# One attention kernel, heads taken in pairs: half-array products, transposed output rows, reciprocals spread by TensorE

## What is computed

```python
dots = einsum('bqhe,bse->bqhs', q_idx, k_idx)                 # indexer, 16 heads of 64
score = where(key_chunk <= q_chunk, sum_h w_h * relu(dots / 8), -inf)
_, sel = top_k(score, 256)
logits = einsum('bqhd,bqkhd->bqhk', q, k[sel]) * 64 ** -0.5   # 8 heads of 64
p = softmax(where(valid, logits, -1e30))
y_a = einsum('bqhk,bqkhd->bqhd', p, v[sel])
x = x + gt1 * (concatenate([y_a, y_b], -1) @ w_o)
h = rmsnorm(x, g_norm_ffn) * (1 + sc2) + sh2                  # then the router and the experts
```

## Time and profile before

| | |
|---|---|
| median of 3 runs | 1916.66 us (1916.6 to 1916.66) |
| the profiled execution | 1921.34 us |
| its span | 1919.2 us |
| TensorE busy | 1657.2 us (86%) |
| VectorE busy | 1389.6 us (72%) |
| ScalarE busy | 724.3 us (38%) |
| mean granted clock | 0.933 |
| attention, first query-key product to the last multiply by the reciprocals | 802.8 to 1186.1 us |

### The profile page before, as it was taken

How to read it: one execution, slowest core, us unless ns; L and a number is a source line. 1 busy time by engine, 2 the same in 40 slices (tenths; PEclk the granted TensorE clock), 3 DMA queues, 4 the chain that set the end, 5 groups by cost and what they waited for, 6 DMA issues and landing times.

```text
span 1919.2 us, 19711 instructions
## 1 busy us (share of the span) xinstructions
PE 1657.2 (86%) x6542; PEld 1090.3 (57%) x6542; DVE 1389.6 (72%) x1888; ACT 724.3 (38%) x819; POOL 170.6 (9%) x173
## 2 busy tenths in 40 slices
PE   2899999999999999468889998359999999999950
PEld 1346554444445545444555666248888888888840
DVE  6323776899778888886655322559999999999948
ACT  4000563000001001121332333037777777777733
POOL 0000000000111111100000000021101101101015
PEclk8899999999999999689999997669999999999985
DMA  9039202200100000672210101079999999999947
GB/s 363 1 132 377 111 1 88 82 14 36 44 6 6 6 12 6 222 257 99 78 49 17 44 28 44 22 291 423 422 411 414 414 412 415 414 414 411 400 161 257
DMA packets 85358, 355.29 MB, mean 185 GB/s; under 512 B 7984, under 2 KB 12208, under 8 KB 60720
## 3 DMA queue, kind: packets, MB, share of 16 engines
q1 hardware_dynamic: 56496, 268.51, 35.3%
q0 software_dynamic: 11776, 44.04, 6.2%
q10 hardware_dynamic: 17024, 41.95, 5.7%
HBM read 295.75 MB, written 58.72 MB: 185 GB/s over the span
## 4 chain that ended last, share of the span: by engine, by line
PE 45%; DVE 7%; ACT 2%; DMA 2%; issue 1%; POOL 0%; POOLq 0%; DVEq 0%; ACTq 0%
PE PS L1610 9%; PE PS L1612 9%; PE PS L1611 9%; PE PS L1572 5%; PE PS L1526 3%; PE PS L1516 3%; PE PS L1605 1%; PE PS L1546 1%; PE PS L1582 1%; DVE wlo L1295 1%; PE PS L1629 1%; ACT WK L730 1%; DVE WK L994 1%; DVE raw L1354 1%; DVE BIG L994 1%
## 5 line engine op out<-in xcount | busy, mean ns | idle before, releaser
L1295 DVE TENSOR_TENSOR wlo<-raw,whi 128x2048 fp32r<-128x2048 f32 x192 | 436.1, 2287 | 45.5 <-ACT whi L757 45.5
L757 ACT ACTIVATE whi<-raw 128x2048 fp32r<-128x2048 f32 x192 | 363.4, 1911 | 56.5 <-DVE WK L1314 45.6
L1414 PE MATMUL PS<-BIG 128*128 128x512 f32 (+1 forms) x768 | 297.5, 543 | 8.6 <-DVE BIG L888 7.5
L1493 PE MATMUL PS<-BIG 128*128 128x512 f32 x512 | 221.6, 593 | 1.4 <-DMA BIG<-in_w_in 0.7
L1414 PEld LDWEIGHTS PS<-BIG 128*128 128x128 f32 x768 | 134.9, 192 | 150.2 <-issue 148.2
L1610 PE MATMUL PS<-whi,xhi 128*128 128x512 f32 x512 | 203.4, 397 | 7.3 <-DVE wlo L1295 6.5
L1612 PE MATMUL PS<-whi,xlo 128*128 128x512 f32 x512 | 200.5, 392 | 0.0
L1611 PE MATMUL PS<-wlo,xhi 128*128 128x512 f32 x512 | 199.9, 390 | 0.0
L973 DVE MAX8 m<-KV 128x8 f32<-128x384 f32 (+5 forms) x192 | 171.6, 894 | 6.0
L974 DVE MATCH_REPLACE8 KV<-m,KV 128x384 f32<-128x384 f32 (+5 forms) x192 | 168.1, 875 | 0.0
L1493 PEld LDWEIGHTS PS<-BIG 128*128 128x128 f32 x512 | 96.7, 190 | 121.7 <-issue 118.6
(11 more groups left out here) (243 smaller groups left out, 2118.9 us busy)
## 6 DMA issues: line engine op xcount, KB each, us to landing
raw<-in_w_gate SPq DMA_DIRECT2D x64, 1024.0 KB, 7.6
raw<-in_w_up SPq DMA_DIRECT2D x64, 1024.0 KB, 7.7
raw<-in_w_down SPq DMA_DIRECT2D x64, 1024.0 KB, 6.8
y_dram<-zero ACTq DMA_DIRECT2D x8, 3072.0 KB, 14.2
BIG<-in_w_in SPq DMA_DIRECT2D x9, 2048.0 KB, 8.7
BIG<-in_w_ada POOLq DMA_DIRECT2D x8, 2048.0 KB, 9.3
y_dram<-WK ACTq DMA_DIRECT2D x32, 512.0 KB, 7.5
BIG<-in_w_ada SPq DMA_DIRECT2D x4, 2048.0 KB, 20.6
```

The lines of the kernel that those rows point to most:

```text
L757: nc.scalar.activation(whi[:, slot], raw[:, q], ACT.Copy).then_inc(G("m_hi"), 1)
L1295: V.tensor_tensor(wlo[:, slot], raw[:, q], whi[:, slot].bitcast(F32), ALU.subtract)\
L1414: last = mm(PS[:, u % 4, 0:w], hT[:, k, tile(t)], ring[n % 2][:, k, 0:w], start=(k == 0), stop=(k == KD - 1))
L1493: last = mm(PS[:, k, :], hT[:, d, tile(t)], wb[k][:, d, :], start=(d == 0), stop=(d == KD - 1))
```

## The change

Queries are stored without padding, and `query_keys(i, lo)` multiplies both heads of a pair, each with the 64 rows that are its own (rows 0 to 63 and 64 to 127), into separate banks. `values(i, lo, g)` is turned round: 64 value columns are stationary, the turned weights stream (128 columns), and the two heads of a pair write partitions 0 to 63 and 64 to 127 of bank 6, so that y arrives transposed. `PT` has four buffers. ScalarE's exponents of the next pair stand between and behind the copies of this one. The reciprocals can no longer be applied along partitions: at `rows` TensorE spreads them (eight products of a broadcast column of `ssum` with the identity, into bank 7), VectorE copies bank 7 to `yT` and multiplies bank 6 by it. `mix` turns `yb` alone. GpSimd no longer clears the query tiles.

```diff
@@ -217,15 +217,15 @@
...
         WC = work([("sums", (4, 512)), ("S", (3, 1024)), ("PT", (2, 512)),
-                   ("y", (512,)), ("yb", (512,)), ("yT", (8, P)), ("bias01", (256,)), ("wr", (8 * 36,)),
-                   ("sq", (D,))])
-        WC["q"] = BIG[:, 18432:20480].rearrange("p (s n) -> p s n", s=2)
+                   ("yb", (512,)), ("yT", (8, P)), ("h2T", (8, P)), ("sq", (D,))])
+        WC["bias01"] = sb("bias01", [P, 256])[:, :]
+        WC["wr"] = sb("wr", [P, 8 * 36])[:, :]
+        WC["q"] = BIG[:, 18432:19456].rearrange("p (s j n) -> p s j n", s=2, j=4)
+        PT = [WC["PT"][:, 0], WC["PT"][:, 1], BIG[:, 19456:19968], BIG[:, 19968:20480]]
...
-        WC["qBD"] = [WC["q"][:, s].rearrange("p (j h n) -> p j h n", j=4, h=2) for s in range(2)]
...
-        WC["h2T"] = WC["yT"]
@@ -314,6 +314,8 @@
...
             if kind == "late":
...
+            if kind == "rows":
+                uses7.append(("rows", n, 0))
@@ -326,7 +328,11 @@
         def pt_index(i, h, g):
-            return HA * sum(groups(k) for k in range(i)) + h * groups(i) + g
+            return HA * sum(groups(k) for k in range(i)) + (h // 2) * 2 * groups(i) + 2 * g + h % 2
+        def pv_index(i, h, g):
+            return pt_index(i, h, g) // 2
@@ -396,15 +402,12 @@
...
             def load_queries(n):
-                for h in range(2):
-                    sp.dma_start(WC["qBD"][n % 2][64 * h:64 * h + 64, :, h, :],
-                                 q_dram[64 * h:64 * h + 64, :, tile(n)]).then_inc(G(f"ld_q{n % 2}"), 16)
+                sp.dma_start(WC["q"][:, n % 2], q_dram[:, :, tile(n)]).then_inc(G(f"ld_q{n % 2}"), 16)
...
-                    sp.wait_ge(G("q_clear"), 1)
@@ -440,7 +443,7 @@
...
-            sp.wait_ge(G("c_pv"), pt_index(T - 1, HA - 1, groups(T - 1) - 1) + 1)
+            sp.wait_ge(G("c_pv"), pv_index(T - 1, HA - 2, groups(T - 1) - 1) + 1)
@@ -549,7 +552,6 @@
...
-            own(nc.gpsimd.memset(WC["q"], 0.0), G("q_clear"))
@@ -708,29 +710,37 @@
...
+            def exponent(u):
+                i, h = divmod(u, HA)
+                S_ = WC["S"][:, u % 3, 0:cols_of(i)]
+                act.wait_ge(G("c_soft"), u + 1)
+                own.go(A(S_, S_, ACT.Exp, bias=nmax[:, u % 4:u % 4 + 1], scale=-1.0, accum_out=ssum[:, i % 2, h:h + 1]),
+                       G("c_exp"))
...
                 if kind == "heads":
...
-                    for h in range(lo, hi + 1):
-                        u = HA * i + h
-                        if h < hi:
-                            act.wait_ge(G("c_soft"), u + 1)
-                            S_ = WC["S"][:, u % 3, 0:K]
-                            own.go(A(S_, S_, ACT.Exp, bias=nmax[:, u % 4:u % 4 + 1], scale=-1.0,
-                                     accum_out=ssum[:, i % 2, h:h + 1]), G("c_exp"))
-                        if h > lo:
-                            for g in range(groups(i)):
-                                n = pt_index(i, h - 1, g)
-                                w = min(512, K - 512 * g)
-                                act.wait_ge(G("c_tr"), n + 1)
-                                if n >= 2:
-                                    act.wait_ge(G("c_pv"), n - 1)
-                                own.go(A(WC["PT"][:, n % 2, 0:w], PS[:, 4 + n % 2, 0:w], ACT.Copy), G("c_pt"))
+                    u = HA * i + lo
+                    if u == 0:
+                        exponent(0)
+                        exponent(1)
+                    after = [v for v in (u + 2, u + 3) if v < HA * T]
+                    for g in range(groups(i)):
+                        for h in range(lo, hi):
+                            n = pt_index(i, h, g)
+                            w = min(512, K - 512 * g)
+                            act.wait_ge(G("c_tr"), n + 1)
+                            if n >= 4:
+                                act.wait_ge(G("c_pv"), n // 2 - 1)
+                            own.go(A(PT[n % 4][:, 0:w], PS[:, 4 + n % 2, 0:w], ACT.Copy), G("c_pt"))
+                        for v in after if groups(i) == 1 else after[g:g + 1]:
+                            exponent(v)
                 if kind == "mix":
...
-                    own.go(A(WC["yT"], PS[:, 4:6, :].rearrange("p b (k n) -> p (b k) n", k=4), ACT.Copy), G("c_yT"))
+                    own.go(A(WC["yT"][:, 4:8], PS[:, 4, :].rearrange("p (k n) -> p k n", k=4), ACT.Copy), G("c_yT"))
@@ -1150,13 +1160,14 @@
                 if kind == "rows":
...
-                    own(V.reciprocal(ssum[:, i % 2, :], ssum[:, i % 2, :]))
-                    dve.wait_ge(G("c_pv"), pt_index(i, HA - 1, groups(i) - 1) + 1)
+                    own(V.reciprocal(ssum[:, i % 2, :], ssum[:, i % 2, :]), G("c_over"))
...
-                        dve.wait_ge(G("c_ytr"), i)
-                    own(V.tensor_tensor(WC["y"].rearrange("p (h d) -> p h d", h=HA),
-                                        PS[:, 6, :].rearrange("p (h d) -> p h d", h=HA),
-                                        ssum[:, i % 2, :].unsqueeze(2).to_broadcast([P, HA, HD]), ALU.mult), G("c_y"))
+                        dve.wait_ge(G("b7_ready"), at7[("mix", i - 1, 1)] + 1)
+                    dve.wait_ge(G("b7_ready"), at7[("rows", i, 0)] + 1)
+                    dve.wait_ge(G("c_pv"), pv_index(i, HA - 2, groups(i) - 1) + 1)
+                    own(V.tensor_copy(WC["yT"][:, 0:4], PS[:, 7, :].rearrange("p (j n) -> p j n", j=4)), G("b7_free"))
+                    own(V.tensor_tensor(WC["yT"][:, 0:4], PS[:, 6, :].rearrange("p (j n) -> p j n", j=4),
+                                        WC["yT"][:, 0:4], ALU.mult), G("c_y"))
@@ -1504,52 +1515,70 @@
...
-            def query_keys(u):
-                i, h = divmod(u, HA)
+            def query_keys(i, lo):
...
-                if h == 0:
-                    pe.wait_ge(G(f"ld_q{i % 2}"), 32 * (i // 2 + 1))
-                if u >= 2:
-                    pe.wait_ge(G("c_soft"), u - 1)
+                if lo == 0:
+                    pe.wait_ge(G(f"ld_q{i % 2}"), 16 * (i // 2 + 1))
+                if HA * i + lo >= 2:
+                    pe.wait_ge(G("c_soft"), HA * i + lo)
...
-                    last = mm(PS[:, 2 * (u % 2) + b, 0:w], WC["qBD"][i % 2][:, h // 2, h % 2, :],
-                              kaT[:, h // 2, 512 * b:512 * b + w], start=True, stop=True)
-                last.then_inc(G("c_qk"), 1)
-            def values(i, h, g):
+                    for h in (lo, lo + 1):
+                        rows = slice(HD * (h % 2), HD * (h % 2) + HD)
+                        last = mm(PS[:, 2 * (h % 2) + b, 0:w], WC["q"][rows, i % 2, h // 2, :],
+                                  kaT[rows, h // 2, 512 * b:512 * b + w], start=True, stop=True)
+                        if w < 512 or 512 * b + w == K:
+                            last.then_inc(G("c_qk"), 1)
+            def turn_weights(i, h, g):
...
-                pe.wait_ge(G("c_pt"), n + 1)
-                if h == 0 and g == 0 and i >= 1:
+                if g == 0:
+                    pe.wait_ge(G("c_exp"), HA * i + h + 1)
+                if n >= 2:
+                    pe.wait_ge(G("c_pt"), n - 1)
+                for b in range(4 * g, min(4 * g + 4, i + 1)):
+                    last = tr(PS[:, 4 + n % 2, P * (b % 4):P * (b % 4) + P],
+                              WC["S"][:, (HA * i + h) % 3, P * b:P * b + P], ident)
+                last.then_inc(G("c_tr"), 1)
+            def values(i, lo, g):
+                n = pt_index(i, lo, g)
+                pe.wait_ge(G("c_pt"), n + 2)
+                if lo == 0 and g == 0 and i >= 1:
...
-                    last = mm(PS[:, 6, HD * h:HD * h + HD], WC["PT"][:, n % 2, P * (b % 4):P * (b % 4) + P],
-                              va[:, b, HD * h:HD * h + HD], start=(b == 0), stop=(b == i))
+                    for h in (lo, lo + 1):
+                        rows = slice(HD * (h % 2), HD * (h % 2) + HD)
+                        last = mm(PS[rows, 6, P * (h // 2):P * (h // 2) + P], va[:, b, HD * h:HD * h + HD],
+                                  PT[(n + h % 2) % 4][:, P * (b % 4):P * (b % 4) + P], start=(b == 0), stop=(b == i))
...
                 if kind == "heads":
...
-                        query_keys(0)
-                        query_keys(1)
-                    todo = None
-                    for h in range(lo, hi):
-                        if HA * i + h + 2 < HA * T:
-                            query_keys(HA * i + h + 2)
-                        for g in range(groups(i)):
-                            n = pt_index(i, h, g)
-                            pe.wait_ge(G("c_exp"), HA * i + h + 1)
-                            if n >= 2:
-                                pe.wait_ge(G("c_pt"), n - 1)
-                            for b in range(4 * g, min(4 * g + 4, i + 1)):
-                                last = tr(PS[:, 4 + n % 2, P * (b % 4):P * (b % 4) + P],
-                                          WC["S"][:, (HA * i + h) % 3, P * b:P * b + P], ident)
-                            last.then_inc(G("c_tr"), 1)
```

(29 more changed lines are left out.)

## The result

The changed kernel takes 1930.4 us (median of 5 runs, 1928.35 to 1936.5) against 1916.66 (1916.6 to 1917.71): the ratio is 1.008, with a 95% interval of 1.0059 to 1.01. It is 13.7 us slower, inside the range given, but on the other side of the likeliest value.

What follows compares the result with a forecast made beforehand. TensorE's path was taken to bound the attention rows, other engines only where it waits. Terms: 33.2 + 5.1 + 1.0 - 12.4 - 6 - 4.5 - 1 - 3 - 8 = 4.4 saved; forecast 1912 us, range 1898 to 1936.

Steps and rivals of the forecast that it cites:

- Pairs: TensorE's query-key products, transposes and values per head pair: n = 8 falls from 9.23 to 7.13 us; 33.2 saved in all.
- Case A: Half-array products overlap, one slot lost at each turn; query-key n = 8 takes 2.14 us; total 1912; chance 0.38.
- case B: Half-array products overlap fully, no slot lost; 8.6 us less, chain takes 2.2 back; total 1905; chance 0.20.
- the sign that I had named: Query-key pair of n = 8 taking 1.7, 2.1 or 3.4 us would show B, A or C; otherwise than A, prediction wrong.
- Cases C and D: C: halves don't overlap, 1931, chance 0.17. D: only one product kind overlaps, 1926 or 1930, chance 0.12.
- Changes of tile form: TensorE drains at three changes a pair, up to 0.17 us each; 3 lost in all.
- The norm's chain: Rows 3 to 7: moved exponent waits on norm and logits, delaying copies and TensorE 2.2 to 2.8 us a row; 12.4 lost.
- The clock: Low-clock stretches behind new idle in five rows: 12.5 us lost less 4.5 of the present one, 8 lost.
- Case E: Clock falls in heads of rows 3 to 7; up to 27 us more than Case A, about 1926; chance 0.13.
- Reciprocals: TensorE's spread products at row ends: 6 us lost over six rows, 4.5 at the first rows, 1.0 after row 7.
- Row 2: Early exponents shorten the stall of 3.71 us behind row 1's mix; with its row's added wait, 1.0 saved.
- Mixing: First y transposes to projection: four transposes instead of eight, 1.30 us instead of 2.15; 5.1 saved over six rows.

Runs made afterwards that it cites:

- experiment 1: Changed kernel, but in row 6 VectorE computes the negated logits of heads 2 and 3 before the rest of the late sums; 1919.94 us, ratio to before 1.0015.
- Experiment 3: Changed kernel plus three unused 512-column products before the third pair's last values in rows 4 to 7; 1921.43 us, ratio 1.0013.

## Why the prediction was wrong, step by step

**Pairs, right in sum, between cases A and B in kind.** Case A gave up a slot at each turn; none is lost. Query-key products of n = 8 take 1.92, of n = 6 1052.22 - 1050.73 = 1.49 (timeline of the kernel after, row 5):

```profile
1050.73 1.56 PE L1529 MATMUL PS<-KV,BIG 64*128 64x512 f32 x8
1052.22 1.09 PE L1542 MATMUL PS<-cst,WK 128*128 128x128 f32 x8
...
1056.10 1.56 PE L1529 MATMUL PS<-KV,BIG 64*128 64x512 f32 x8
```

Halved streaming alone, case B, gives 1.72 and 1.29, case A 2.14 and 1.71; both are 0.20 above B's, and so are n = 4, 5 and 7 (1.06, 1.28, 1.71). Pairs take 7.02 (put at 7.13), 6.12 for n = 7 (6.4; read in experiment 1, where that pair has no wait), 1056.10 - 1050.73 = 5.37 (5.6), 5.38 for n = 5 (4.9; two single transposes wait for their bank there) and 4.22 for n = 4 (4.06). Against the pairs before this saves 2.2 x 3 + 0.9, 2.07 x 4, 2.17 x 4, 1.51 x 4 and 0.17 x 4: 31.2, with the changes of form in it. The 0.9 is an estimate for the last pair of row 7 at equal clocks: it took 10.16 before at the low clock (1174.96 to 1185.12), 5.08 if halved, and takes 4.19 at the full clock in experiment 1 (1178.26 to 1182.45). I had 33.2 less 3, with 2.7 for that pair, the clock in it. By the sign that I had named, the halves do behave otherwise than in A. Cases C and D are ruled out; that the 1930.4 measured is so near what they gave (1931, and 1926 or 1930) is chance.

**Changes of tile form, right.** A pair's query-key products cost 0.20 more than half of the streaming. I had a bound of 0.17 for each change, which 0.20 is just above. That the 0.20 is the change of form is my reading; nothing separates it from a start-up of the half arrays.

**The norm's chain, right.** It was to cost 2.2 to 2.8 in each of rows 4 to 7 and 2.4 in row 3. Timeline of TensorE, row 3, after:

```profile
965.35 1.09 PE L1383 MATMUL PS<-cst,WK 128*128 128x128 f32 x8 [1.47 <-DVE WK L1192]
968.54 3.62 PE L1609 MATMUL PS<-wr,WK 128*128 128x36 f32 x16 [2.10 <-ACT WK L752]
```

The gaps of rows 4 to 7 are 2.67, 2.70, 2.72 and 2.74; row 3 has 1.47 and 2.10 - 1.11, 2.5. Together 13.3 for the 12.4 of the sum.

**The step that failed: a missing term.** I costed an exponent that is moved ahead of copies by one of VectorE's delays, that which recurs in every row, and did not go through VectorE's list for others. The prediction speaks of the late sums in rows 0 and 1 only. Their remainder in row 6 lies between logits and logits, and experiment 1 puts it at 10.5: with it the sum is 6.1 lost instead of 4.4 saved. This step alone turns the sign of the sum. It is not all of the 18 us between the forecast and the result.

**The clock, net about right, by errors that cancel.** 12.5 lost less 4.5 given back was the term. Experiment 3 gave 9 back behind the gaps of rows 4 to 7, and the low clock that stayed in these rows isn't in it. Row 3 was not filled: by the table its stretch (projection of row 2 to that of row 3) is 4.5 longer, of which the other terms make 0.7, so I put 3.8 down to its clock. Given back were 3.6, all in row 7, which falls short of the full clock by 0.13 x 52 = 6.8 us where it was 0.18 x 58 = 10.4; row 4 stands at 0.89 for 0.90. So 9.2 stand for the net 8, apart from the 3.8 behind row 6's first pair. A bound from the stretches: rows 3 to 7 fall short by 0.15 x 46 + 0.11 x 48 + 0.19 x 62 + 0.09 x 54 + 0.13 x 52 = 35.6 us, against 0.10 x 53 + 0.18 x 58 = 15.7 before, and some of the 20 between them fell on idle time. Case E had the right cause and too large a price.

**Reciprocals, right.** In rows 0 and 1 TensorE waits as described, and at the ends of later rows the products take 0.98 (1143.37 - 1142.39, row 6), for the 1.0 of the sum. Timeline, after, row 0:

```profile
822.82 1.97 PE L1579 MATMUL PS<-cst,ssum 128*64 128x128 f32 x16 [2.03 <-DVE ssum L1163]
```

At the low clock sixteen records take 1.9, as I put it. The projection of row 0 ends only 2.2 later than before (L1182 at 870.22, L1171 at 868.02), that of row 1, behind the other row's reciprocals, 4.4 later: 4.5 was the term for both rows.

**Row 2, wrong.** Here I had put 1.0 saved. The stall of 3.71 did shrink, to the 2.87 before the values at 921.98. But the norm's transposes now wait 1.98 (924.83), and the router behind takes 3.62 instead of 1.98: I had the norm's chain from row 3 on only. From the projection of row 1 to that of row 2 the kernel after needs 3.7 more. No experiment takes this row by itself.

**Mixing, right.** Timeline, after, row 7, transposes and projection, for the earlier trace rows:

```profile
1150.24 0.66 PE L1592 MATMUL PS<-cst,WK 128*128 128x128 f32 x4
1151.58 7.13 PE L1599 MATMUL PS<-BIG,WK 128*128 128x512 f32 x16 [0.69 <-ACT WK L743]
```

1.34 where 1.30 was put and 2.15 stood.

**The sum with measured terms.** 31.2 + 5.1 - 13.3 (chain) - 10.5 (row 6) - 9.2 (clock) - 5.8 (reciprocals of six rows) - 4.4 (rows 0 and 1) - 3.5 (row 2, without the mixing and reciprocals already counted) - 1 (end) = 11.4 lost, and the spans are 9.2 apart. The 2.2 too many have no place of their own; the 3.8 and the 3.5 are themselves read off by subtraction. The medians differ by 13.7, 4.5 more than the two profiled executions: the one before was 4.7 above its median, that after stood at it.

## What to carry to other kernels

When an instruction is moved forward on an engine that runs its list in order, everything behind it inherits the lateness of what it waits for: go through the whole list of the engine that supplies it, with one-off work such as a remainder that is worked off at one place, and price each delay, not only the one that recurs. The early exponents cost more than they brought here, since the values that needed them came a pair later, while the copies behind it were due at once. And a short wait costs more than its length if the products behind it then run at half the clock, so remove waits before counting streamed columns.

The kernel that keeps the half-array products and puts ScalarE back in its old order is the best of all measured: 1885.41 and 1886.0 us (1883.49 with the query-key products in series), 1.7% less than the kernel before.

## What the runs showed of the hardware that I had not expected

- **Two half arrays run as two streams.** Products in the two row halves take half of their streaming time and 0.20 us; 128-column records in the two column halves start 0.055 apart (16 records in 1.09 less the last one's 0.27), full-array transposes of the same width 0.107, and records that stand later in the program, for one half, start between those that stand earlier, for the other. Whether heads alternate matters for nothing in the query-key products (1883.49 against 1885.41) and for 12.6 us with the values.
- **Adding products made the kernel faster.** 10 us of unused products cost nothing in the gaps and gave 9 us back behind them. In row 7, from the last values of the third pair on, the granted clock is 0.53 in the kernel after (1182 to 1193 us) and 0.84 with the fill (1176 to 1187, since this kernel is 6.2 earlier there; first line after, second with the fill):

```profile
1182.00:1193.00 11.00, 9.89 (x56) 8.70 (x54) 0.40 (x2) 3.52 (x6) 0.00 (x0) 0.53 0.00 1
```

```profile
1176.00:1187.00 11.00, 9.89 (x102) 8.80 (x98) 0.40 (x2) 4.13 (x7) 0.00 (x0) 0.84 0.01 1
```
